# Weight ring of a mixture-of-experts step: nine aligned slot pairs in place of eight pairs between two single slots, and block 12 of the first pass beside the ring in two halves

## The reference

```
x = x + mixer(rms_norm(x))
logits = rms_norm(x) @ w_router + b_router ; top 4 of 32, softmax gates
for each expert e, on the tokens routed to it:
    gu = h @ w_gate_up[e] + b_gate_up[e]          # w_gate_up: 32 x 1024 x 2048
    act = (clip(up) + 1) * (gate * sigmoid(1.702 * gate))
    y += gate_weight * (act @ w_down[e] + b_down[e])   # w_down: 32 x 1024 x 1024
y = rms_norm(x + y)
```

## Time and profile before

| | us |
|---|---|
| median of three runs | 1218.33 (1217.04 to 1218.47) |
| the profiled execution | 1216.78 |
| its span, first to last instruction | 1214.8 |
| TensorE busy | 1174.4 (97%) |
| VectorE, ScalarE, GpSimd busy | 392.1, 232.5, 83.3 |
| first expert matmul / last one's end | 286.5 / 1202.8 |

### The profile page before, as it was taken

One profiled execution on the slowest core, in us unless ns is written; L12 is line 12 of the kernel. 1 busy time (PEld: TensorE's weight loads), 2 busy tenths in 40 slices (PEclk: granted clock), 3 DMA queues, 4 the chain that ended last, 5 costly groups with the idle time before them and its releaser, 6 DMA issues.

```text
span 1214.8 us, 16286 instructions
## 1 busy us (share of the span) xinstructions
PE 1174.4 (97%) x6511; PEld 666.8 (55%) x6511; DVE 392.1 (32%) x665; ACT 232.5 (19%) x398; POOL 83.3 (7%) x243
## 2 busy tenths in 40 slices
PE   9999999999999999899999989999999998999997
PEld 7999999985535354343434343535435343553533
DVE  4648587654252413021211111121212111221213
ACT  5533783233101010000101010101101010110102
POOL 4100000010101001101100010101011010110000
PEclk9999999999999999899999999999999999999999
DMA  6543336589999999999999999999999999999995
GB/s 232 169 161 106 102 139 233 205 320 374 421 426 427 426 426 427 422 429 426 424 429 426 427 424 420 421 424 427 426 428 426 427 425 428 425 427 426 427 423 229
DMA packets 54735, 443.70 MB, mean 365 GB/s; under 512 B 5340, under 2 KB 5436, under 8 KB 23680
## 3 DMA queue, kind: packets, MB, share of 16 engines
q1 hardware_dynamic: 53296, 439.91, 87.8%
q0 software_dynamic: 1216, 2.68, 0.9%
q10 hardware_dynamic: 144, 0.04, 0.0%
HBM read 440.63 MB, written 1.98 MB: 364 GB/s over the span
## 4 chain that ended last, share of the span: by engine, by line
PE 86%; DMA 11%; issue 1%; DVE 1%; ACT 0%; POOLq 0%; POOL 0%; ACTq 0%; DVEq 0%; SPq 0%
PE ps L1739 31%; PE ps L1807 18%; DMA wexp<-in_w_gate_up_dram 10%; PE ps L1631 7%; PE ps L1368 7%; PE ps L1370 7%; PE ps L1369 7%; PE ps L1647 2%; PE ps L1648 1%; PE ps L1681 1%; PE ps L1751 1%; PE ps L1639 1%; DMA rows<-in_conv_w_dram 1%; PE ps L1593 0%; PE ps L1686 0%
## 5 line engine op out<-in xcount | busy, mean ns | idle before, releaser
L1739 PE MATMUL ps<-wexp,xt 128*64 128x512 f32 (+1 forms) x2048 | 460.2, 602 | 18.4 <-DMA wexp<-in_w_gate_up_dram 13.0
L1739 PEld LDWEIGHTS ps<-wexp,xt 128*64 128x64 f32 (+1 forms) x2048 | 143.8, 132 | 262.4 <-issue 261.6
L1807 PE MATMUL ps<-wexp,act_t 128*64 128x512 f32 (+1 forms) x1104 | 227.0, 593 | 4.2 <-issue 4.2
L1807 PEld LDWEIGHTS ps<-wexp,act_t 128*64 128x64 f32 (+1 forms) x1104 | 82.0, 131 | 134.2 <-issue 134.1
L1272 DVE TENSOR_TENSOR y<-y,ps 128x1024 f32<-128x1024 f32 x51 | 60.8, 1219 | 209.3 <-PE ps L1648 200.4
L837 ACT ACTIVATE g<-g 128x512 f32<-128x512 f32 x33 | 20.8, 630 | 545.8 <-DVE g L1286 545.8
L1368 PE MATMUL ps<-act_h,split 128*128 128x384 f32 x352 | 117.8, 335 | 0.0
L1370 PE MATMUL ps<-act_h,split 128*128 128x384 f32 x352 | 117.6, 334 | 0.0
L1369 PE MATMUL ps<-act_l,split 128*128 128x384 f32 x352 | 117.6, 334 | 0.0
L1631 PEld LDWEIGHTS ps<-pick,xn 128*128 128x128 f32 x768 | 91.1, 196 | 14.8 <-issue 14.8
L1631 PE MATMUL ps<-pick,xn 128*128 128x128 f32 x768 | 94.1, 283 | 1.7 <-POOL pick L588 1.7
(11 more groups left out here) (326 smaller groups left out, 970.8 us busy)
## 6 DMA issues: line engine op xcount, KB each, us to landing
wexp<-in_w_gate_up_dram SPq DMA_DIRECT2D x92, 2048.0 KB, 25.3
wexp<-in_w_down_dram SPq DMA_DIRECT2D x48, 2048.0 KB, 26.8
wexp<-in_w_gate_up_dram SPq DMA_DIRECT2D x38, 1024.0 KB, 25.8
wexp<-in_w_down_dram SPq DMA_DIRECT2D x20, 1024.0 KB, 12.5
raw<-in_w_in_dram SPq DMA_DIRECT2D x19, 1024.0 KB, 5.1
wexp_low<-in_w_gate_up_dram SPq DMA_DIRECT2D x17, 1024.0 KB, 25.5
wexp_high<-in_w_gate_up_dram SPq DMA_DIRECT2D x16, 1024.0 KB, 23.9
wexp_low<-in_w_down_dram SPq DMA_DIRECT2D x5, 1024.0 KB, 21.8
```

Source lines behind the costliest of these rows:

```text
L1739: i_ = pe.matmul(ps[s0:s0 + w, b, :], xt[:, k, s0:s0 + w], weights(k, x)[:, at_:at_ + UC], start=k == 0, stop=k == CB - 1)
L1807: i_ = pe.matmul(ps[s0:s0 + w, 6 + c, :], act_, weights(CB + m, x)[:, D * kk + UC * c:D * kk + UC * c + UC], start=k == 0, stop=k == CB - 1)
```

## The change

It puts the ring at nine aligned pairs. `RING_AT` has 18 addresses, nine pairs of adjacent ones, with a new pair at 106496 and 114688 in the positions 6 and 7. `wexp_low`, `wexp_high`, the branch of two DMAs (L440 to L443) and `second_landed` go away. A unit begins at `PLACES[i]` = `LOADS[i]`, an even place. The first unit keeps its places, and so ends at place 22; place 23 (`SKIPPED`) stays empty in that lap.

The block beside the ring is now in two buffers of 4 KB a partition, its gate columns at 205824 and its up columns at 176128, the addresses where u (`u1`) and the transposed activations (`act_t`) are put later. `g1`, `u1`, `out_h`, `out_l`, `bias_hl`, `bdn_hl`, `state_out` move to make room. The first half is loaded where `beside` was; the second, after SP's wait for `order_ready`, which now stands ahead of it and of blocks 19 and 20.

Block 0 is no longer loaded at `PB_U`: blocks 0 to 3 take the four stages that held 1 to 4, and each later point issues blocks one further on. Four go out at `mrg_ready` in place of two. Block 18 goes out with 15, 16 and 17, and the late load behind `combined` is gone. For the second unit's pairs the count to wait for comes from `ring_of`: - 18 + 2, but - 17 + 2 for places 30 to 39. The blocks of the third unit and all after it wait for the same counts as before.

```diff
-RING_AT = (65536, 73728, 81920, 90112, 155648, 163840, 49152, 57344, 0, 8192, 16384, 24576, 32768, 40960, 139264, 147456)
-RING_AT = (201728,) + RING_AT + (118784,)
+RING_AT = (65536, 73728, 81920, 90112, 155648, 163840, 106496, 114688, 49152, 57344, 0, 8192, 16384, 24576, 32768, 40960, 139264, 147456)
...
-PLACES = [n_ - 1 for n_ in LOADS]
+PLACES = LOADS
+SKIPPED = PLACES[1] - 1
...
+def ring_of(place):
+
+    return RINGS - 1 if RINGS + BESIDE <= place < RINGS + SKIPPED - 1 else RINGS
...
-        beside = at("beside", 106496, [P, 2 * D])
+        beside = [at("beside_gate", 205824, [P, D]), at("beside_up", 176128, [P, D])]
...
             sp.wait_ge(stored, 5 * 16)
-            sp.dma_start(beside[:], exp_one(BESIDE % 2, BESIDE // 2)).then_inc(beside_landed, 16)
+            load_beside(0)
             sp.wait_ge(unit_used, MIX_U - 1)
-            load_expert(11)
             load_expert(13)
+            load_expert(14)
             sp.wait_ge(unit_used, MIX_U)
-            for n in range(14, RINGS):
+            for n in range(15, RINGS + 1):
                 load_expert(n)
 
+            sp.wait_ge(order_ready, 1)
+            load_beside(1)
             for n in range(RINGS + 1, RINGS + 3):
                 sp.wait_ge(wexp_used, n - RINGS)
                 load_expert(n)
-            sp.wait_ge(order_ready, 1)
...
-                    m, x, slot = n // 2 // len(ids), n // 2 % len(ids), (unit + n - 1) % RINGS
+                    m, x, slot = n // 2 // len(ids), n // 2 % len(ids), (unit + n) % RINGS
                     sp.wait_ge(wexp_used, later + (unit + n - ring(n) + 2))
...
-                    if slot == RINGS - 1:
-                        sp.dma_start(wexp[slot][:], exp_two(ids[x], m)[:, 0:2 * D]).then_inc(exp_landed[slot], 16)
-                        sp.dma_start(wexp[0][:], exp_two(ids[x], m)[:, 2 * D:4 * D]).then_inc(exp_landed[0], 16)
-                        continue
...
-            def early_ring(unit):
-
-                return lambda n: RINGS + 1 if unit + n < RINGS + BESIDE else RINGS
-
-            load_pass(LOADS[1], 0, second, early_ring(LOADS[1]), end=8)
-            sp.wait_ge(combined, TT)
-            load_expert(RINGS)
-            load_pass(LOADS[1], 0, second, early_ring(LOADS[1]), begin=8)
+            load_pass(LOADS[1], 0, second, lambda n: ring_of(LOADS[1] + n))
```

More of the change, by code:

```diff
@@ L94, in landings @@
 def landings(place):
-    if place % 2 == 1 or place % RINGS == 0:
+    if place % 2 == 0:
         return place // RINGS + 1
-    return sum(1 for f in FINE for q in range(PLACES[f], min(PLACES[f + 1], place + 1)) if q >= 0 and q % RINGS == place % RINGS)
+    return sum(1 for f in FINE for q in range(PLACES[f], min(PLACES[f + 1], place + 1)) if q != SKIPPED and q % RINGS == place % RINGS)
 def first_place(n):
     return n if n < BESIDE else n - 1
+def ring_of(place):
+    return RINGS - 1 if RINGS + BESIDE <= place < RINGS + SKIPPED - 1 else RINGS
 def strips(shape):
@@ L142, in hawk_gmlp_moe_streaming_step @@
         raw = at("raw", 49152, [P, MIX_RING, KB, UC])
-        wtwo = [at(f"wexp{i}", offset, [P, 4 * D]) for i, offset in enumerate(RING_AT[1:RINGS - 1:2])]
+        wtwo = [at(f"wexp{i}", offset, [P, 4 * D]) for i, offset in enumerate(RING_AT[0::2])]
         wexp = [w[:, 2 * D * i:2 * D * i + 2 * D] for w in wtwo for i in range(2)]
-        wexp = [at("wexp_low", RING_AT[0], [P, 2 * D])] + wexp + [at("wexp_high", RING_AT[-1], [P, 2 * D])]
-        beside = at("beside", 106496, [P, 2 * D])
+        beside = [at("beside_gate", 205824, [P, D]), at("beside_up", 176128, [P, D])]
         x_in = at("x_in", 126976, [P, TT, D])
@@ L155, in hawk_gmlp_moe_streaming_step @@
         tmp = at("tmp", 94208, [P, CB // 2, T])
-        state_out = at("state_out", 106496, [36, D])
+        state_out = at("state_out", 205824, [36, D])
         act_h = at("act_h", 102400, [P, CB, T], F32R)
@@ L159, in hawk_gmlp_moe_streaming_step @@
         xt = at("xt", 102400, [P, CB, P])
[L160 to L163, removed]
+        g1 = at("g1", 201728, [P, 2, UC])
+        u1 = at("u1", 205824, [P, 2, UC])
+        out_h = at("out_h", 201728, [P, D], F32R)
+        out_l = at("out_l", 205824, [P, D], F32R)
         ga = at("ga", 126976, [P, CB, T])
@@ L171, in hawk_gmlp_moe_streaming_step @@
         scale = at("scale", 139264, [P, TT, P])
-        bias_hl = at("bias_hl", 114688, [P, D], F32R)
+        bias_hl = at("bias_hl", 122880, [P, D], F32R)
         bdn = at("bdn", 184320, [3 * NE, D])
-        bdn_hl = at("bdn_hl", 122880, [3 * NE, D], F32R)
+        bdn_hl = at("bdn_hl", 201728, [3 * NE, D], F32R)
         gate_b = at("gate_b", 163840, [P, CB, T])
@@ L262, in hawk_gmlp_moe_streaming_step @@
         exp_landed = [sem(f"exp_landed{i}") for i in range(RINGS)]
-        beside_landed = sem("beside_landed")
         last_landed = [[sem(f"last_landed{k}{x}") for x in range(2)] for k in range(2)]
@@ L283, in hawk_gmlp_moe_streaming_step @@
         mult_used = sem("mult_used")
+        beside_landed = sem("beside_landed")
         st_packed, st_turned, st_ready = sem("st_packed"), sem("st_turned"), sem("st_ready")
@@ L365, in load_expert, with load_beside @@
                 sp.dma_start(wexp[slot][:], exp_one(n % 2, n // 2)).then_inc(exp_landed[slot], 16)
+            def load_beside(h):
+                sp.dma_start(beside[h][:], exp_one(BESIDE % 2, BESIDE // 2)[:, D * h:D * h + D]).then_inc(beside_landed, 16)
             for n in range(MIX_U):
@@ L385, in _ @@
                     sp.wait_ge(st_packed, 2)
-                    load_expert((n - PA_U - 1) // 2 + 1)
+                    load_expert((n - PA_U - 1) // 2)
             sp.wait_ge(yb_ready, 1)
@@ L392, in _ @@
             sp.wait_ge(mrg_ready, CB)
-            load_expert(5)
-            load_expert(6)
+            for n in range(4, 8):
+                load_expert(n)
             sp.wait_ge(low_done, MIX_U - 1)
-            load_expert(7)
+            load_expert(8)
             sp.wait_ge(low_done, MIX_U)
-            load_expert(8)
+            load_expert(9)
             sp.wait_ge(unit_used, MIX_U - 2)
-            load_expert(9)
             load_expert(10)
+            load_expert(11)
             sp.wait_ge(st_ready, 1)
@@ L453, in _ @@
                 load_expert(n)
-            def early_ring(unit):
-                return lambda n: RINGS + 1 if unit + n < RINGS + BESIDE else RINGS
-            load_pass(LOADS[1], 0, second, early_ring(LOADS[1]), end=8)
-            sp.wait_ge(combined, TT)
-            load_expert(RINGS)
-            load_pass(LOADS[1], 0, second, early_ring(LOADS[1]), begin=8)
+            load_pass(LOADS[1], 0, second, lambda n: ring_of(LOADS[1] + n))
             for it in range(2, OVER_AT):
-                load_pass(LOADS[it], 0, ranked(it), early_ring(LOADS[it]))
+                load_pass(LOADS[it], 0, ranked(it), lambda n: RINGS)
             sp.wait_ge(table_ready, 1)
@@ L1694, in place, with weights @@
                     return unit + experts * k + x if fine else unit + 2 * (experts * (k // 2) + x) + k % 2
-                def weights(k, x):
+                def weights(k, x, at_):
                     if first and experts * k + x == BESIDE:
-                        return beside
-                    return wexp[place(k, x) % RINGS]
+                        return beside[at_ // D][:, at_ % D:at_ % D + UC]
+                    return wexp[place(k, x) % RINGS][:, at_:at_ + UC]
                 def landed(k):
@@ L1705, in landed @@
                         if first and experts * k + x == BESIDE:
-                            pe.wait_ge(beside_landed, 16)
+                            pe.wait_ge(beside_landed, 2 * 16)
                             continue
@@ L1709, in landed @@
                         pe.wait_ge(exp_landed[slot], later * 16 + count if later is not None and slot in OVER_SLOTS else count)
[L1711 to L1715, removed]
                 half = shape is HALF
@@ L1725, in experts_pass @@
                         landed(k)
-                    else:
-                        second_landed(k)
                     if last and k == CB - 1:
@@ L1739, in experts_pass @@
                             i_ = pe.matmul(ps[s0:s0 + w, b, :], xt[:, k, s0:s0 + w],
-                                           weights(k, x)[:, at_:at_ + UC], start=k == 0, stop=k == CB - 1)
+                                           weights(k, x, at_), start=k == 0, stop=k == CB - 1)
                             if k == CB - 1 and b == 2 and (n == 0 if half else n == len(strips(shape)) - 1):
@@ L1794, in experts_pass @@
                         landed(CB + m)
-                    else:
-                        second_landed(CB + m)
                     by_columns = last and m == CB // 2 - 1
@@ L1806, in experts_pass @@
                             act_ = act_t[:, k % 4, SLOTS * (k // 4):SLOTS * (k // 4) + SLOTS] if half else act_t[:, k, s0:s0 + w]
```

(2 more changed lines are left out.)

3 lines of the change are left out of this document (removed).

## The result

| | before | after |
|---|---|---|
| median, us | 1217.77 (1216.54 to 1220.94) | 1220.85 (1219.97 to 1221.51) |
| span of the profiled execution, us | 1214.8 | 1218.3 |
| first expert matmul, us | 286.5 | 285.98 |

The change makes the kernel slower: ratio 1.0025, 95% interval 1.0018 to 1.0031, that is 3.0 us (2.2 to 3.8). The forecast was + 3.9, with a likeliest band of + 3.1 to + 5.4, so the difference lies at that band's lower edge. The median before is of 20 runs now, 0.56 us under the three that the prediction had.

The account below looks back on a forecast made before the run. The prediction took bytes moved by the DMA engines to set the end: 1216.78 + 4.9 (gap) - 1.0 (whole pairs) = 1220.7 us profiled, and 1222.2 with 1.55 added for the median. The range was 1218 to 1225.

Parts of the forecast that it names:

- What bounds the kernel: From 343 us to the last loads: DMA engines never idle, so bytes moved by a given time set the end.
- The counts: Second unit's loads: with `wexp_used` at 16, 32 blocks issued after the change in place of 34 before.
- The idle stretch: Before 331 us, DMA engines idle some 5.4 us, with no issues between 318.3 and 329.6.
- the gap: At 331 us, loads stand two blocks behind the kernel before, adding 4.9 us, bounds 4.4 and 5.4.
- The last wait: At the last unit's start, TensorE's final wait for loads ends 4.9 us later, near 1154.
- one block more ahead of the state stores: At the front, one more queued block delays the first half beside to about 270.4 from 267.90 us, without cost.
- The term given back: 18 split pairs become single DMAs, saving 0.035 us a block, 1.3 us in all; 1.0 taken, lower bound 0.
- a whole pair's landing among the rivals: At another pair's last wait, whole landing comes up to 2.46 us later; within the slower-still rival, chance 0.11.
- The rival of the clock with a late pair: At the end, slow clock and late whole pair together give 1226; within the slower-still rival, chance 0.11.
- The clock rival: After the last wait, TensorE's first matmuls run slower, adding 1.8 us: 1224.0; slower-still chance 0.11.

Follow-up runs that it names:

- e1: Changed kernel with the second unit's five pairs at places 30 to 39 each issued as two one-block loads; 1218.66 us, ratio 1.0013 to the kernel before.
- e4: Changed kernel with the second unit's blocks 30 to 37 waiting for a count two higher again; 1224.94 us, ratio 1.0068 to the kernel before.
- e2: Kernel before with blocks 30 to 39 waiting for a count of consumed blocks two higher; 1221.41 us, ratio 1.0037 to the kernel before.
- e6: Changed kernel with the `order_ready` wait and second half of the block beside moved behind blocks 19 and 20; 1220.77 us, ratio 1.0027 to before.
- e3: Changed kernel without the block beside the ring, so no straddled pair or empty place; 1217.53 and 1216.76 us, ratios 0.9999 and 0.9991 to before.
- e5: e3 with every pair outside the one-block units issued as two one-block loads; 1227.90 us, ratio 1.0087 to the kernel before.
- e8: e3 with the last unit's pairs not already specially loaded issued as single blocks in step order; 1215.63 us, ratio 0.9989 to before.

## Why the prediction was right

**What bounds the kernel: right.** The end follows the DMA engines' bytes at 345 us. This is shown, by taking bytes away in four doses; in three of them (e1, the change, e4) TensorE's row near the hole is 39.74 us as before, and only in e2 did TensorE wait there.

**The counts: right.** In the changed kernel nothing is issued between the pair at 317.82 us and the one at 329.10, and data flow again at 330.0 us, where the prediction had 331. The idle stretch was forecast as 5.4 us, and the gap, two blocks, as 4.9. The hole amounts to 4.7 us (2.0 MB); up to 345 us, against the kernel before, 4.6 are missing. The last wait ends at 1153.0, forecast near 1154.

**A wrong count that cost nothing.** I had one block more ahead of the state stores and the first half of the block beside at 270.4 us. From the mixer's last stage on, two blocks more are queued there (eight against six), and it went out at 272.55. That is still ahead of the next wait, which ended at 273.94. As all that was issued has drained by 330 us, the front's details don't reach the end; e6 shows it for the order wait, too.

**The term given back: right in size, and a term forgotten beside it.** The 0.035 us a block hold, so 36 blocks are 1.3 us where I took 1.0. But I looked for the seam only at the last wait of the kernel before, and found it was not there. I didn't ask which pair would be late next. The seam also stood on the last unit's second down pair (the last row, at 1158.3), where TensorE was about to wait; made whole, it lands for its first step with its second, and 0.7 us are lost in the changed kernel's profile. I had a whole pair's landing among the rivals, at up to 2.46 us, with a small chance and not in the sum. The sum should have been + 4.6 - 1.3 + 0.7 = 4.0. That this is so near the forecast's 3.9 is luck: the gap 0.3 too large, the giving back 0.3 too small and the 0.7 left out cancel. The profiled spans differ by 3.5 us and the first expert matmul came 0.5 us earlier after (TensorE waited 0.7 us less for its first loads, at the start of the kernel, which the change doesn't touch): 4.0. So the terms add up within the two profiles. The medians differ by 3.1 and the ratio says 2.2 to 3.8, so about 1 us stays unexplained. All terms but the second are read from one profile each, and such readings move by as much: the first wait for loads by 0.7 us, the last waits in e3 by 2.5. (The rival of the clock with a late pair should have read 1226.5, 1224.0 + 2.46, not 1226.)

**The clock rival.** One unit after a wait took 8.75 us for its first 32 matmuls (1034.07), as in the earlier trace rows, at a mean granted clock of 0.81 from 1034 to 1043 us. But the last unit's first 16, after a wait too, took 3.65 at 1.00, as in the earlier trace rows. It played no part at the end.

## What to carry to other kernels

When a saturated DMA queue sets the end, look for the moment when it last runs nearly dry and count the bytes issued up to it, before and after; what was issued early and has drained by then was worth nothing here. A ring that loads in pairs wants both slots of a pair freed by the same step: a block taken out of the ring shifts all behind it by one, and costs a slot for as long as the pairs straddle. Large loads stream a little faster, but where the consumer is about to wait, a pair in two halves lets it start on the first; taking the block beside out of the ring and splitting that one pair gave 0.9988 and 0.9987 to the kernel before, against 1.0025 for the change.

## What the runs showed of the hardware

Where 1 MiB loads follow each other in a full queue, SP is held up while it issues them. From 345 us on an issue took 1.92 us in the median in e5 and up to 4.90, and two in e8 took 6.0 and 6.2, against 0.33 in the median for a pair (the changed kernel). Already in the kernel before, those of the one-block units' gate/up loads took 1.92 in the median and up to 4.31. The longest time from issue to landing falls from 36.8 us in e3 to 28.5 in e5, while the median stays (26.8 and 26.3). A queue that takes a limited number of pieces would do this, as it holds fewer bytes of smaller loads; no run tests it. Nor was it separated from the loads' size as the reason of the rate: a queue of 2 MiB loads runs at 427 GB/s and one of 1 MiB loads at 421, at the same busy share of 1.01 (e3, e5). The share alone would call both saturated, and doesn't show 1.4% of the bandwidth.

From an issue on SP into an empty queue to the first bytes it was 0.9 to 1.0 us (329.10 to 330.0 in the changed kernel, 274.45 to 275.4 in the one before).

TensorE at full clock can be busy 39.74 of 40 us while the DMA engines fall 9.4 us behind beside it (e4). That loss appears only later, as waits at the starts of units: the first one for DMA comes after 600 us in the kernel before, between 550 and 600 in the changed one, and between 450 and 480 in e4.
